# Scale and shift in quarters between the pool mixer's weights, and small loads earlier in the queue

## The reference

```python
mod_x = (jax.nn.silu(c) @ w_mod[l] + b_mod[l])[:, None, :]
mod_c = jax.nn.silu(c_ctx) @ w_mod[l] + b_mod[l]
sh1, sc1, gt1, sh2, sc2, gt2 = jnp.split(mod_x, N_MOD, axis=-1)
csh1, csc1, cgt1, csh2, csc2, cgt2 = jnp.split(mod_c, N_MOD, axis=-1)
h_x = _modulate(x, g_pre_mix[l], sh1, sc1)       # rmsnorm(x) * (1 + sc1) + sh1
h_c = _modulate(ctx, g_pre_mix[l], csh1, csc1)
u_x, q_x, k_x, v_x = _project(h_x, w_in[l])      # columns of h @ w_in, 512 each
u_c, q_c, k_c, v_c = _project(h_c, w_in[l])
attn_x = _neighbourhood_attention(q_x, k_x, v_x, k_c, v_c, rpb[l])
mix_x = jnp.concatenate([_pool_mixer(u_x, pool_w[l], pool_scale[l]), attn_x], axis=-1) @ w_out[l]
```

## Time and profile before

| | us |
|---|---|
| median of three runs | 962.33 |
| the three runs | 962.33, 955.25, 962.38 |
| the profiled execution, its own time | 960.95 |
| its span | 959.1 |
| PE busy in it | 883.9 |

### The profile page before, as it was taken

How to read it: one execution, slowest core, us unless ns; L and a number is a source line. 1 busy time by engine, 2 the same in 40 slices (tenths; PEclk the granted TensorE clock), 3 DMA queues, 4 the chain that set the end, 5 groups by cost and what they waited for, 6 DMA issues and landing times.

```text
span 959.1 us, 13869 instructions
## 1 busy us (share of the span) xinstructions
PE 883.9 (92%) x5354; PEld 743.0 (77%) x5354; DVE 522.6 (54%) x892; ACT 444.4 (46%) x788; POOL 44.5 (5%) x55
## 2 busy tenths in 40 slices
PE   6795998997999999979999999899889899999996
PEld 2583784555999999759999999787556589999995
DVE  1530525547677555566555555677446565555554
ACT  2541224436554555355444444566445654444443
POOL 1000000000000000000000000045110000000000
PEclk9798798998999999999999999999779999999998
DMA  9868572202588666535665566485102156666631
GB/s 365 320 223 326 222 286 67 66 23 88 169 267 273 216 193 178 166 104 201 192 193 180 181 191 177 126 284 188 33 3 91 62 180 208 184 179 195 184 102 44
DMA packets 45104, 166.14 MB, mean 173 GB/s; under 512 B 4976, under 2 KB 5104, under 8 KB 44784
## 3 DMA queue, kind: packets, MB, share of 16 engines
q1 hardware_dynamic: 45040, 165.26, 52.7%
HBM read 164.19 MB, written 1.05 MB: 172 GB/s over the span
## 4 chain that ended last, share of the span: by engine, by line
PE 85%; DVE 4%; DMA 3%; ACT 3%; issue 3%; POOL 1%; SPq 0%; DVEq 0%; ACTq 0%; POOLq 0%
PE ps L1336 12%; PE ps L1338 12%; PE ps L1337 12%; PE ps L1356 12%; PE ps L1358 11%; PE ps L1360 11%; PE ps L1497 3%; DMA raw<-in_w_mod_p 2%; PE ps L1379 2%; PE ps L1511 1%; PE ps L1481 1%; PE ps L1389 1%; DMA big<-in_invcnt 1%; DVE lo L853 1%; ACT hi L439 1%
## 5 line engine op out<-in xcount | busy, mean ns | idle before, releaser
L853 DVE TENSOR_TENSOR lo<-raw,hi 128x1024 fp32r<-128x1024 f32 (+1 forms) x247 | 299.2, 1218 | 200.8 <-ACT hi L439 200.6
L439 ACT ACTIVATE hi<-raw 128x1024 fp32r<-128x1024 f32 (+1 forms) x247 | 256.9, 1048 | 114.0 <-PE ps L1360 63.1
L1336 PE MATMUL ps<-Th,hi 128*128 128x256 f32 (+1 forms) x960 | 278.1, 290 | 15.5 <-DVE lo L853 12.6
L1338 PE MATMUL ps<-Th,lo 128*128 128x256 f32 (+1 forms) x960 | 276.9, 288 | 0.0
L1337 PE MATMUL ps<-Tl,hi 128*128 128x256 f32 (+1 forms) x960 | 276.9, 288 | 0.0
L1336 PEld LDWEIGHTS ps<-Th,hi 128*128 128x128 f32 x960 | 185.4, 193 | 23.2 <-issue 19.3
L1356 PE MATMUL ps<-hi,Th 128*128 128x512 f32 (+2 forms) x524 | 181.3, 405 | 8.3 <-DVE lo L853 5.5
L1337 PEld LDWEIGHTS ps<-Tl,hi 128*128 128x128 f32 x960 | 185.5, 193 | 3.8
L1338 PEld LDWEIGHTS ps<-Th,lo 128*128 128x128 f32 x960 | 185.3, 193 | 1.6
L1358 PE MATMUL ps<-lo,Th 128*128 128x512 f32 (+2 forms) x524 | 176.2, 395 | 0.0
L1360 PE MATMUL ps<-hi,Tl 128*128 128x512 f32 (+2 forms) x524 | 175.7, 394 | 0.0
(11 more groups left out here) (170 smaller groups left out, 597.8 us busy)
## 6 DMA issues: line engine op xcount, KB each, us to landing
raw<-in_ffn_down SPq DMA_DIRECT2D x44, 512.0 KB, 4.1
raw<-in_w_mod_p SPq DMA_DIRECT2D x40, 512.0 KB, 6.9
raw<-in_ffn_gate SPq DMA_DIRECT2D x40, 512.0 KB, 3.7
raw<-in_ffn_up SPq DMA_DIRECT2D x40, 512.0 KB, 3.5
raw<-in_w_mlp_out SPq DMA_DIRECT2D x32, 512.0 KB, 4.6
raw<-in_w_mlp_in SPq DMA_DIRECT2D x28, 512.0 KB, 4.2
raw<-in_w_out SPq DMA_DIRECT2D x16, 512.0 KB, 6.2
raw<-in_w_in_q SPq DMA_DIRECT2D x8, 512.0 KB, 4.8
```

The lines of the kernel that those rows point to most:

```text
L439: e.activation(hi[h % RING][:, 0:w], raw[n % RAW][:, 0:w], ACT.Copy).then_inc(s_hi, 1)
L853: e.tensor_tensor(lo[h % RING][:, 0:w], raw[n % RAW][:, 0:w], hi[h % RING][:, 0:w], ALU.subtract).then_inc(s_lo, 1)
L1336: e.matmul(o, a, Th[:, k, c0:c1], start=(k == 0), stop=False)
L1338: return e.matmul(o, b, Th[:, k, c0:c1], start=False, stop=(k == KT - 1))
```

## The change

The plan interleaves: four pieces of w_mod_p, then one of u, four times. w_mod_p is reordered, so that four pieces hold one quarter (256 columns) of the scale and the same quarter of the shift, for x and the context. For each quarter, ACT alone copies one bank (quarter_part), PE turns it (quarter_turned), DVE makes that quarter of modc and A1 (quarter_columns, three operations), and ACT scales and shifts two blocks of 128 in one operation each and writes their Th (first_turned), DVE their Tl (first_low). Then both engines split u_j. DVE has no part in the scaling of x any more, and doesn't copy half rows for scale and shift. PE runs u's products block by block, as quarters come, between the mod products. The context's eight blocks go through the same functions: PE transposes groups 0 and 1 after q0, groups 2 and 3 after q1; ACT and DVE do all four groups after uT(3), that is, behind the split of q3. Of the small loads, x is issued before the first piece, invcnt together with ctx before q0, the late columns before k0, bias1 before k3. The diff, cut to its core:

```diff
-    s = c[0:12] + u[0:1] + c[12:14] + u[1:2] + c[14:16] + u[2:4]
+    s = []
+    for j in range(4):
+        s += c[4 * j:4 * j + 4] + u[j:j + 1]
     for j in range(4):
...
-                if n == 2:
+                if n == 0:
                     e.dma_start(x[:, :, :], t["x"].rearrange("(i p) d -> p i d", p=P)).then_inc(s_x, 16)
                 if n == CH_AT["w_in_q", 0]:
                     e.dma_start(cx, t["ctx"].rearrange("(i p) d -> p i d", p=P)).then_inc(s_cx, 16)
-                if n == H[11]:
                     e.dma_start(big[:, 10432:11456], t["invcnt"].partition_broadcast(P)).then_inc(s_inv, 16)
-                if n == H[13]:
+                if n == CH_AT["w_in_k", 0]:
                     e.dma_start(cols[:, EARLY:], t["cols"][:, EARLY:]).then_inc(s_late, 16)
-                if n == H[15]:
+                if n == CH_AT["w_in_k", 3]:
                     e.wait_ge(s_xTp, 8)
                     e.dma_start(arena[:, 0:4096], t["bias1"]).then_inc(s_b1, 16)
...
+            def quarter_part(j):
+
+                e.wait_ge(s_whole, 4 * j + 4)
+                if j >= 2:
+                    e.wait_ge(s_rowT, j - 1)
+                e.activation(rows_of(PT[0], j % 2), ps[j % 2][:, :], ACT.Copy).then_inc(s_rowA, 1)
+
+            def first_turned(c, j):
+
+                n0, sl = 8 * c + 2 * j, slice(c * L, (c + 1) * L)
+                if c == 0:
+                    e.wait_ge(s_mod, 3 * j + 3)
+                e.wait_ge(s_xTp, 4 * c + j + 1)
+                for k in (2 * j, 2 * j + 1):
+                    e.activation(xT[:, k, sl], ps[2 + j % 2][:, (k % 2) * L:(k % 2 + 1) * L], ACT.Identity,
+                                 bias=modc[:, 2 * k + c:2 * k + c + 1],
+                                 scale=A1[:, 2 * k + c:2 * k + c + 1]).then_inc(s_xTa, 1)
+                for k in (2 * j, 2 * j + 1):
+                    e.wait_ge(s_xTa, 8 * c + k + 1)
+                    e.activation(Th[:, k, sl], xT[:, k, sl], ACT.Copy).then_inc(s_Th1, 1)
...
             first_norm(1)
-            mod_part(0)
-            first_turned(0)
-            first_turned(2)
-            split(1)
-            mod_part(1)
-            e.wait_ge(s_mod, 3)
-            e.wait_ge(s_xTa, 4)
-            for k in range(KT):
-                if k == 2:
-                    e.wait_ge(s_xTd, 2)
-                if k == 6:
-                    e.wait_ge(s_xTd, 4)
-                e.activation(Th[:, k, 0:L], xT[:, k, 0:L], ACT.Identity,
-                             bias=modc[:, 2 * k:2 * k + 1]).then_inc(s_Th1, 1)
-            split(3)
+            for j in range(4):
+                quarter_part(j)
+                first_turned(0, j)
+                split(j)
             first_norm(2)
             first_norm(3)
             split(4)
...
-                if g == 2:
-                    ctx_turned(0)
-                    ctx_turned(1)
                 if g == 3:
-                    ctx_turned(2)
-                    ctx_turned(3)
+                    for j in range(4):
+                        first_turned(1, j)
                 split(h + RING)
...
+            def quarter_columns(j):
+
+                sl, bl, at = slice(4 * j, 4 * j + 4), slice(2 * j, 2 * j + 2), ps[j % 2]
+                e.wait_ge(s_rowT, j + 1)
+                e.tensor_tensor(pairs(modc[:, sl]), pairs(at[:, 4:8]), twice(col("b_sh1")[:, bl]),
+                                ALU.add).then_inc(s_mod, 1)
+                e.wait_ge(s_sc1b, 1)
+                e.tensor_tensor(pairs(A1[:, sl]), pairs(at[:, 0:4]), twice(sc1b[:, bl]), ALU.add).then_inc(s_mod, 1)
+                e.wait_ge(s_mod, 3 * j + 2)
+                e.tensor_tensor(pairs(A1[:, sl]), pairs(A1[:, sl]), twice(col("g_mix")[:, bl]),
+                                ALU.mult).then_inc(s_mod, 1)
+
+            def first_low(c, j):
+                sl = slice(c * L, (c + 1) * L)
+                for k in (2 * j, 2 * j + 1):
+                    e.wait_ge(s_Th1, 8 * c + k + 1)
+                    e.tensor_tensor(Tl[:, k, sl], xT[:, k, sl], Th[:, k, sl], ALU.subtract).then_inc(s_T1, 1)
...
+            for j in range(4):
+                quarter_columns(j)
+                first_low(0, j)
+                split(j)
...
-                if g == 2:
-                    ctx_low(0)
-                    ctx_low(1)
                 if g == 3:
-                    ctx_low(2)
-                    ctx_low(3)
+                    for j in range(4):
+                        first_low(1, j)
                 split(CH["w_in_u", g] + RING)
...
+                if v < 2:
+                    bank, c0 = n // 4 % 2, n % 4 // 2 * L
+                else:
+                    bank += quarter // 2
                 e.wait_ge(s_raw[at % RAW], lands(at))
-                if n % 8 == 0 and v == 2:
-                    e.wait_ge(s_mod, 2)
-                if n % 8 == 0 and v == 3:
-                    e.wait_ge(s_mod, 3)
-                    e.wait_ge(s_xTa, 12)
-                if n % 8 == 0 and v == 4:
-                    e.wait_ge(s_rowA, 3)
-                    e.wait_ge(s_rowD, 3)
+                if n in (8, 12):
+                    e.wait_ge(s_mod, 3 * (n // 4) - 3)
+                if n == 16:
+                    e.wait_ge(s_mod, 12)
+                if n == 24:
+                    e.wait_ge(s_xTa, 16)
+                if n == 32:
+                    e.wait_ge(s_rowA, 5)
+                    e.wait_ge(s_rowD, 1)
...
+            def quarter_turned(j):
+
+                src = rows_of(PT[0], j % 2)
+                e.wait_ge(s_rowA, j + 1)
+                for b in range(4):
+                    m = e.matmul(ps[j % 2][:, 2 * b:2 * b + 2], src[:, b * P:(b + 1) * P], col("sel"), start=True,
                                  stop=True)
                 m.then_inc(s_rowT, 1)
...
+                if 4 * c + j >= 2:
+                    e.wait_ge(s_xTa, 2 * (4 * c + j - 1))
+                for k in (2 * j, 2 * j + 1):
...
+            def u_blocks(g, k0, k1):
+
+                split_ready(CH["w_in_u", g])
+                for k in range(k0, k1):
+                    if g == 0:
+                        e.wait_ge(s_T1, k + 1)
+                    m = wstat_k(CH["w_in_u", g], ROT[g], 0, L, k)
+                if k1 == KT:
+                    m.then_inc(s_used, 1)
+
             e.wait_ge(s_cols, 16)
             e.wait_ge(s_silu, 1)
-            for n in range(16):
-                mod_product(n)
-                if 4 <= n < 8:
-                    turn_rows(0, n - 4, n)
-                if n == 9:
-                    mod_turned(0, 0, 0, col("sel"))
-            mod_turned(1, 2, 0, col("sel"))
-
-
-            e.wait_ge(s_xTa, 4)
-            e.wait_ge(s_xTd, 4)
+            for j in range(4):
+                mod_product(4 * j)
+                mod_product(4 * j + 1)
+                if j >= 2:
+                    u_blocks(j - 1, 0, 2 * j - 2)
+                mod_product(4 * j + 2)
+                mod_product(4 * j + 3)
+                turn_rows(0, j)
+                if j:
+                    u_blocks(0, 2 * j - 2, 2 * j)
+                quarter_turned(j)
+                for g in range(1, j):
+                    u_blocks(g, 2 * j - 2, 2 * j)
             for g in range(4):
-                h = CH["w_in_u", g]
-                split_ready(h)
-                for k in range(KT):
-                    if g == 0:
-                        e.wait_ge(s_T1, k + 1)
-                    m = wstat_k(h, ROT[g], 0, L, k)
-                m.then_inc(s_used, 1)
-                if g == 2:
-                    e.wait_ge(s_mod, 3)
-                    turn_rows(1, 0, 2)
-                    turn_rows(1, 1, 3)
+                u_blocks(g, 6 if g < 3 else 0, KT)
+
+
             for a in range(4):
                 e.wait_ge(s_u, a + 1)
                 wstat(CH["w_in_q", a], ROT[a], 0, L)
                 if a == 0:
-                    turn_rows(1, 2, 2)
-                    turn_rows(1, 3, 3)
+                    turn_rows(1, 0)
+                    turn_rows(1, 1)
+                if a == 1:
+                    turn_rows(1, 2)
+                    turn_rows(1, 3)
                 for n in range(16 + 2 * a, 18 + 2 * a):
...
-        "w_mod_p": np.concatenate([_quarters(w_mod[:, a:a + 1024]) for a in (1024, 0, 2048, 3072, 4096)]),
+        "w_mod_p": np.concatenate([
+            np.stack([_quarters(w_mod[:, a:a + 1024]).reshape(4, 2, P, 1024) for a in (1024, 0)],
+                     axis=1).reshape(16, P, 1024)] +
+            [_quarters(w_mod[:, a:a + 1024]) for a in (2048, 3072, 4096)]),
```

More of the change, by code:

```diff
@@ L153, in build @@
         flat = [PT[i][:, :, :].rearrange("p a b -> p (a b)") for i in range(2)]
-        part = [flat[0], acc, flat[0], flat[1], acc]
+        part = [None, None, flat[0], flat[1], acc]
         srcs = [x[:, 0, :], x[:, 1, :], cx[:, 0, :], cx[:, 1, :]]
@@ L255, in build @@
         ROT = [4, 5, 6, 7]
-        MODB = [0, 2, 0, 2, 0]
+        MODB = [None, None, 0, 2, 0]
         FB = [[0, 1], [2, 3]]
@@ L314, in twice @@
```

(56 more changed lines are left out.)

38 lines of the change are left out of this document (7 added, 31 removed).

## The result

| | us |
|---|---|
| kernel before, median of 15 runs | 956.78 (952.92 to 962.38) |
| changed kernel, median of 15 runs | 962.66 (958.95 to 967.40) |
| ratio, changed to before | 1.0053, 95% interval 1.0027 to 1.0079 |
| the profiled execution of the changed kernel | 962.50, span 960.6 |

By the ratio the change costs 5.1 us, 2.6 to 7.5 by the interval; the two medians differ by 5.9. The forecast was +5.8. As an absolute time it said 966.8 us, 4.1 above the median, because it started from a profiled execution of 960.95 us, and the median of 15 runs is 956.78.

A forecast was written before the change was run, and what follows sets the result against it. PE, busy 92% of the span, was taken as the bound, gains coming only from its idle time or slow clock. +0.1 + 9.3 - 3.6 = +5.8 on 960.95 gave 966.8 us, range 957 to 973.

The forecast's parts named there:

- U: The end of u3's products on PE, forecast at 52.3 us, before 52.2.
- Stage A: From the start up to U: quarters overlap but are chained through the splits, +0.1 us (ends -3.8 to +2.1).
- Stage B: From U to k0's start, 17.7 us before: waits in the q stage add 9.3 us (ends +6.9 to +10.8).
- q0's lo: Term of Stage B: q0's lo stands on DVE behind the context's scaling, so PE waits 1.65 us.
- the wait for q3: Term of Stage B: PE's context transposes wait 4.1 us after q1, as ACT's scaling stands behind q3's split.
- The clock's term: Term of Stage B: the waits lower PE's clock, and restarting costs 2.2 us.
- Stage C: From k0 to v's first product, 48.8 us before: the invcnt wait goes, -3.6 us (ends -6.2 to -1.5).
- What is late next: In Stage C, without the invcnt wait: k2's load, k2 10.0 us after k1's start, then k3 behind bias1.
- (1): Rival: k3 and bias1 come in time, Stage C gives -13 us, total 957.4 us; chance 0.12.
- (2): Rival: no wait for q3, c17's slot comes free early, 7.4 us less in Stage B, 959.4 us; chance 0.09.
- (3): Rival: low clock through all of Stage A, U at 59.4, sum +13, 974 us; chance 0.16.
- (4): Rival: all quarters hidden behind the loads, U at 41.5, sum -23.7, 937 us; chance 0.03.

The follow-up runs named there:

- experiment 2: Changed kernel with bias1 issued ahead of v3 again, not ahead of k3: ratio to the kernel before 0.9953.
- experiment 10: Changed kernel with the late columns issued ahead of v1 again, not ahead of k0: ratio to the kernel before 1.0056.
- experiment 5: Changed kernel with PE's order altered, each quarter's four mod products, transposes and turning before u's blocks: ratio to the kernel before 1.0012.
- experiment 1: Changed kernel with the first two context groups ahead of the split of q3 again on ACT and DVE: ratio to the kernel before 0.9990.
- experiment 8: Experiment 7's kernel with the late columns ahead of v1 again and q0 split before the context's norms: ratio to the kernel before 0.9833.
- experiment 7: Changed kernel with the edits of experiment 1, experiment 2 and experiment 5 together: ratio to the kernel before 0.9888.
- experiment 3: Kernel before with only the changed places of x, invcnt, late columns and bias1: ratio to the kernel before 0.9990.
- experiment 6: Kernel before with invcnt alone moved, issued with ctx ahead of q0: ratio to the kernel before 0.9895.
- experiment 4: Changed kernel with the small loads at their old places: ratio to the kernel before 1.0082.

## Why the prediction was right

**The sum.** +5.8 was forecast, +5.1 measured. Up to v the profiled executions differ by 3.1 us only, 2.7 under the forecast, which the interval of the ratio (2.6 to 7.5 us) just holds. The time agrees with the sum better than the trace does, and that the sum came within a microsecond is in part luck: each stage has terms that were a microsecond or so off, and it is +3.2 that the three stages of this trace add up to. A single trace can't settle the difference. The kernels of experiments 2 and 10 need 27.3 and 27.4 us from U to k0, against 25.8 in this trace and 27.0 forecast, and a v 1.5 us later would bring the trace to 4.6, close to the time.

**Stage A, +0.1 forecast, -2.1 measured.** The chain is there, where the prediction put it, and experiment 5 shows that it was PE's order. Its links were sized too long. The first quarter's turning ran at the high clock (1.0, not 1.8 us). From a turned quarter to a ready lo it took 4.3, not 4.65 us (31.70 to 36.03). The fourth quarter took 6.3 us from its wait to its turning, not 7.2, as the clock was low for less of it. Two terms were off, then: the clock by 0.8 and 0.9 us, and the link by 0.3 us in each of four quarters; 0.2 of that are DVE's three column operations of a quarter's width, done in 0.46 us (31.74 to ACT's start at 32.20), not 0.65.

On the clock, each of the two longer waits was followed by the low clock, as the products at 26.96 and 37.97 show. But it came about a microsecond into the burst (the blocks at 26.05 and 36.09 began fast) and was over before its end, and after the wait of 0.90 at 44.84 there was none. Half of a burst at the low clock was what the forecast had taken; it was about half in the third quarter (5.65 us, 5.8 forecast) and less in the fourth. The rule that the prediction drew on, in the Trainium skill, "TensorE: Matmul & The Clock Gate", section "HAM oscillation — how this bites in real kernels", is about bursts shorter than the waits between them. The bursts here last 7.5 and 7.8 us (26.05 to 33.5, 36.09 to 43.9) behind waits of 3.16 and 2.57, so its condition isn't met, and the prediction was wrong to read out of it that all blocks of this stage would be slow; this trace neither bears the rule out nor refutes it.

**Stage B, +9.3 forecast, +8.1 measured.** Term by term: q0's lo 1.65 against 1.22; the wait for q3 4.1 against 3.74; the second group 1.15 against 0.89; the clock 2.2 against about 1.5 (0.9 at the products of 65.64, the rest at the transposes before and the first block behind). The clock's term is the one that another execution changes: in experiment 2, with the same code, the clock stayed low until 71 us, not 68, and U to k0 took 27.3. Experiment 1 shows the cause of the two waits after q1. That q0's lo is late behind the context's norms is read from the traces (ACT works on them from 45.38 to 47.84 in this one) and has no experiment of its own: experiment 8 moves them, but in experiments 5 and 7, where they stand as before, q0's wait is down to 0.2 us too. The late columns cost nothing in this kernel, as forecast (experiment 10), and 1.1 us where nothing hides k0's load (experiment 3, which moves the other small loads as well), for which the range had 1.5.

**Stage C, -3.6 forecast, -2.8 measured.** "What is late next" was right twice: k2 10.7 us after k1 (forecast 10.0), k3 26.9 (25.2), PE idle 2.22 and 6.13. The pieces ahead of k3 came later than at one per 1.28 us from the first slot: the split of k3 began 24.4 us after k1's start, where 22.6 was worked out. The queue was busy meanwhile: from 92 to 107.8 us the windows view has it at 407 GB/s, which is 12.3 pieces' worth, where eleven lead up to k3. So loads issued behind k3, from 102.03 on, were moving before k3 was usable; 1.3 pieces at 1.28 us would account for the time, but which bytes moved when isn't shown, and the cause stays open. k3 to v gave 0.9 us back (11.6, not 12.5). The place of bias1 is confirmed by experiments 2, 3 and 6 from both sides; experiment 2 gave 8.0, where the working has five for the load and up to 2.6 for the clock.

**The rivals.** (1), bias1 in time: refuted at 110.26, by PE's wait of 6.13 us for k3's lo. It had v 28.3 us after k1; even with bias1 out of the way (experiment 2) it is 30.5. (2), no wait for q3: refuted at 63.11. (3), low clock throughout: refuted, U at 50.1. (4) fell with the waits at 26.05 and 36.09; with the products first (experiment 5) U is 44.8, where it had 41.5, and with five edits (experiment 8) the design reaches v at 104.1.

## What to carry to other kernels

Cutting a producer into quarters gains only if the consumer of a quarter doesn't stand ahead of the next quarter's products in any engine's written order; with the products first the same cut paid (U at 44.8 to 46.9 us, against 48.9 to 50.5). When a wait for a small load is removed, ask which load is next in the same queue before moving another ahead of it: the early invcnt alone was worth 10 us, and 2 MB put ahead of k3 took most of it (k1 to v 9.2 us shorter in experiment 6, 2.6 in experiment 3). And what one engine needs from another should not stand behind a wait for a load there: the context's scaling behind q3's split cost 4 us and more.

## What the runs showed of the hardware

Identical work after v's start took different times. From v to the end it is 840.3 us in the kernel before, 838.7 in the changed one, 840.5 and 840.6 in experiments 4 and 5, and 835.3 to 836.5 in the eight others. The instructions are the same. Counted from the end, the executions part in several places. Some 2.5 of the 5 us between experiments 4 and 1 arise between 283 and 265 us before the end, in the second attention stage: the windows view of 60 us that begin some 285 us before the end has the clock at 0.78 with 206 matmuls in experiment 4, and at 0.81 with 215 in experiment 1:

```profile
682.50:742.50 60.00, 52.35 (x206) 35.07 (x204) 29.29 (x121) 29.72 (x88) 6.25 (x8) 0.78 0.09 29
```

```profile
667.00:727.00 60.00, 53.19 (x215) 35.40 (x215) 31.43 (x132) 30.83 (x92) 6.92 (x10) 0.81 0.13 38
```

The 15 times of the kernel before that stand in the table of results seem to fall into two groups, 952.9 to 957.6 and 960.2 to 962.4. The further 57 that were taken beside the experiments don't bear that out: twelve of them lie between the two. The times spread over ten microseconds, and from one execution little can be told.

The clock takes part in that. Before the same products of k0, a wait of 2.39 us was followed by the high clock (experiment 1), and one of 1.93 us by 3.4 us at the low one (experiment 7, 67.84 to 71.23). After the waits behind q1 the clock was back at 68 us in the changed kernel and at 71 in experiment 2. Before k3, a wait of 2.80 us had no low clock behind it (experiment 2), and waits of 3.04, 3.00 and 2.56 us had (6, 7 and 8).

So a difference of spans between two single executions says little here below 5 us. The start of v leaves out most of that and was the better measure of every edit, but not below some 2 us. It wasn't found what decides which length an execution takes.
